# Moving eight modulation blocks from the norm stops into the FFN loops of a two-model program

## The reference, cut to what matters

```python
m_lat = jnp.split((silu_c @ w_mod[i] + b_mod[i])[:, None, :], N_MOD, axis=-1)      # N_MOD = 9
m_ctx = jnp.split((silu_cc @ w_mod[i] + b_mod[i])[None, None, :], N_MOD, axis=-1)

def swiglu(u, w_in, w_out):
    a, v = jnp.split(u @ w_in, 2, axis=-1)
    return (jax.nn.silu(a) * v) @ w_out

def ffn_sublayer(h, shift, scale, gate, w_in, w_out, g, b):
    y = swiglu(modulate(h, shift, scale), w_in, w_out)
    return layer_norm(ALPHA * h + FFN_RES * gate * y, g, b)

def ada_modulation(cond, w_ada, b_ada):                                            # the second model
    m = (jax.nn.silu(cond) @ w_ada + b_ada)[:, None, :]
    return jnp.split(m, 6, axis=-1)
```

## Time and profile before

| | before |
|---|---|
| median of 3 runs | 2881.59 us (2879.3 to 2887.91) |
| profiled execution, its own time | 2883.8 us |
| its span in the trace | 2882.1 us |
| granted TensorE clock, mean | 0.954 of full |
| PE busy | 2612.0 us, 91% |
| weight loads (beside PE) busy | 1885.5 us, 65% |
| DVE busy | 1523.2 us, 53% |
| ACT busy | 894.8 us, 31% |
| POOL busy | 221.8 us, 8% |
| L1974 splits on DVE | 392, 477.6 us |
| L2013 multiply-adds on DVE | 210, 259.8 us |

### The profile page before, as it was taken

How to read it: one execution, slowest core, us unless ns; L and a number is a source line. 1 busy time by engine, 2 the same in 40 slices (tenths; PEclk the granted TensorE clock), 3 DMA queues, 4 the chain that set the end, 5 groups by cost and what they waited for, 6 DMA issues and landing times. The chain is left out here.

```text
span 2882.1 us, 39680 instructions
## 1 busy us (share of the span) xinstructions
PE 2612.0 (91%) x14422; PEld 1885.5 (65%) x14422; DVE 1523.2 (53%) x2305; ACT 894.8 (31%) x1421; POOL 221.8 (8%) x372
## 2 busy tenths in 40 slices
PE   5999997998999999999999878997988998798987
PEld 3878874665687887687876647996666433466322
DVE  3855754444576576675676556566543232563101
ACT  2222224443322222422224444445333100443100
POOL 0000103231010000100010001000001000000000
PEclk9999998998999999999999989998998999899999
DMA  7655545232475454654555206664104699515998
GB/s 265 195 163 148 171 141 139 73 74 72 148 211 172 137 172 150 210 183 144 162 186 171 66 27 208 187 180 122 56 15 194 285 426 428 177 47 241 405 428 348
DMA packets 428844, 527.78 MB, mean 183 GB/s; under 512 B 29766, under 2 KB 382532, under 8 KB 416292
## 3 DMA queue, kind: packets, MB, share of 16 engines
q1 hardware_dynamic: 393188, 399.71, 40.4%
q0 software_dynamic: 35520, 126.24, 13.8%
HBM read 524.85 MB, written 1.05 MB: 182 GB/s over the span
## 5 line engine op out<-in xcount | busy, mean ns | idle before, releaser
L1974 DVE TENSOR_TENSOR wlo<-raw,whi 128x1024 fp32r<-128x1024 f32 x392 | 477.6, 1222 | 298.0 <-ACT whi L1492 277.2
L1492 ACT ACTIVATE whi<-raw 128x1024 fp32r<-128x1024 f32 x392 | 413.9, 1057 | 588.0 <-PE bank L714 527.2
L712 PE MATMUL bank<-xhi,whi 128*128 128x512 f32 (+1 forms) x1568 | 575.0, 367 | 3.0 <-DVE xlo L2539 3.0
L713 PE MATMUL bank<-xlo,whi 128*128 128x512 f32 (+1 forms) x1568 | 565.8, 361 | 0.0
L714 PE MATMUL bank<-xhi,wlo 128*128 128x512 f32 (+1 forms) x1568 | 565.2, 360 | 0.0
L712 PEld LDWEIGHTS bank<-xhi,whi 128*128 128x128 f32 x1568 | 298.3, 190 | 65.5 <-issue 22.4
L714 PEld LDWEIGHTS bank<-xhi,wlo 128*128 128x128 f32 x1568 | 298.1, 190 | 45.1
L713 PEld LDWEIGHTS bank<-xlo,whi 128*128 128x128 f32 x1568 | 298.7, 191 | 43.5 <-issue 0.7
L2013 DVE SCALAR_TENSOR_TENSOR acc<-mod_ring,conds,acc 128x1024 f32<-128x1024 f32 x210 | 259.8, 1279 | 7.7 <-DMA mod_ring<-in_w_ada 3.4
L1368 PE MATMUL bank<-experts,gathered 128*64 128x512 f32 (+1 forms) x1024 | 236.6, 617 | 28.9 <-DMA experts<-in_w_up 25.9
L712 PE MATMUL bank<-hhi,whi 128*128 128x512 f32 (+1 forms) x704 | 256.4, 364 | 0.2 <-DVE hlo L2121 0.2
(11 more groups left out here) (323 smaller groups left out, 3363.0 us busy)
## 6 DMA issues: line engine op xcount, KB each, us to landing
raw<-in_ffn_w_in SPq DMA_DIRECT2D x176, 512.0 KB, 4.0
mod_ring<-in_w_mod POOLq DMA_DIRECT2D x128, 512.0 KB, 4.8
experts<-in_w_gate SPq DMA_DIRECT2D x32, 2048.0 KB, 20.7
experts<-in_w_up SPq DMA_DIRECT2D x32, 2048.0 KB, 20.2
experts<-in_w_down SPq DMA_DIRECT2D x32, 2048.0 KB, 21.0
mod_ring<-in_w_ada POOLq DMA_DIRECT2D x96, 512.0 KB, 5.0
raw<-in_ffn_w_out SPq DMA_DIRECT2D x64, 384.0 KB, 3.3
raw<-in_ffn_w_out SPq DMA_DIRECT2D x64, 320.0 KB, 3.2
```

Of the source, the lines that this page charges most:

```text
L712: pe.matmul(o, wh, hi[:, k0 + k, cols], start=(first and k == 0), stop=False)
L713: pe.matmul(o, wh, lo[:, k0 + k, cols], start=False, stop=False)
L1492: act.activation(whi[:, slot, :], raw[:, slot, :], ACT.Copy).then_inc(*n.mark("hi_ready"))
L1974: dve.tensor_tensor(wlo[:, slot, :], raw[:, slot, :], whi[:, slot, :].bitcast(F32), ALU.subtract)\
```

## The change

The fillers are taken out of all engines. Their eight blocks (six of two conditions, two of one) become riders on DVE, most of them in the down loops, which carried none. `RIDERS` now has four lists for each FFN: up and down of half 0, up and down of half 1. A down loop that carries a block is written out as one piece of two or four iterations instead of a hardware loop of four. `SLICES` gets an entry for four repetitions, and blocks of one repetition put their eight slices after the first two splits, four and four. On POOL, the attention bias no longer stands behind 16 filler transfers.

```diff
-RIDERS = (((("w_mod", 0, 2, 2, 2, 2), ("w_ada_2", 1, 3, 1, 1, 1)), (("w_mod", 0, 4, 2, 2, 2), ("w_ada_2", 1, 4, 1, 1, 1))),
-          ((("w_mod", 1, 1, 2, 2, 2), ("w_mod", 1, 7, 1, 1, 1)), (("w_ada_2", 1, 0, 2, 2, 2), ("w_ada_2", 1, 2, 1, 1, 1))),
-          ((("w_ada_2", 0, 0, 2, 2, 2), ("w_mod", 1, 8, 1, 1, 1)), (("w_ada_2", 0, 3, 2, 2, 2), ("w_ada_2", 1, 5, 1, 1, 1))),
-          ((("w_ada_2", 0, 2, 1, 0, 1), ("w_ada_2", 0, 5, 1, 0, 1)), ()))
-SLICES = {1: (3, 3, 2, 0), 2: (1, 2, 1, 2, 1, 1, 0, 0)}
+RIDERS = (
+    ((("w_mod", 0, 2, 2, 2, 2), ("w_ada_2", 1, 3, 1, 1, 1)), (("w_mod", 0, 6, 1, 2, 4),),
+     (("w_mod", 0, 4, 2, 2, 2), ("w_ada_2", 1, 4, 1, 1, 1)), (("w_mod", 0, 7, 1, 2, 4),)),
+    ((("w_mod", 0, 8, 1, 2, 2), ("w_mod", 1, 0, 1, 2, 2), ("w_mod", 1, 7, 1, 1, 1)), (("w_mod", 1, 3, 1, 2, 2), ("w_mod", 1, 5, 1, 1, 2)),
+     (("w_mod", 1, 1, 2, 2, 2), ("w_ada_2", 1, 2, 1, 1, 1)), (("w_mod", 1, 4, 1, 2, 4),)),
+    ((("w_ada_2", 1, 0, 2, 2, 2), ("w_mod", 1, 8, 1, 1, 1)), (("w_ada_2", 0, 3, 1, 2, 2), ("w_mod", 1, 6, 1, 1, 2)),
+     (("w_ada_2", 0, 0, 2, 2, 2), ("w_ada_2", 1, 5, 1, 1, 1)), (("w_ada_2", 0, 4, 1, 2, 4),)),
+    ((("w_ada_2", 0, 2, 1, 0, 1), ("w_ada_2", 0, 5, 1, 0, 1)), (), (), ()))
+SLICES = {1: (4, 4, 0, 0), 2: (1, 2, 1, 2, 1, 1, 0, 0), 4: (1, 0, 1, 0, 1, 1, 0, 1, 0, 1, 1, 0, 1, 0, 0, 0)}
 MACS_AHEAD = 8
-FILLERS = ((("w_mod", 0, 6), ("w_mod", 0, 7)), (("w_mod", 0, 8), ("w_mod", 1, 0)), (("w_mod", 1, 3), ("w_mod", 1, 4)), (("w_mod", 1, 5), ("w_mod", 1, 6)))
...
     yield "up", 0, 0, 1, 1, None
     for half, (_, nf) in enumerate(HALVES):
-        first, last = 1 - half, nf // 2
-        for name, l, block, times, conds, reps in riders[half]:
-            yield "up", half, first, times, reps, (name, l, block, conds)
-            first += times * reps
-        assert first <= last
-        if first < last:
-            yield "up", half, first, last - first, 1, None
-        yield "down", half, 0, KD // 2, 1, None
+        for kind, first, last, ridden in (("up", 1 - half, nf // 2, riders[2 * half]), ("down", 0, KD // 2, riders[2 * half + 1])):
+            for name, l, block, times, conds, reps in ridden:
+                yield kind, half, first, times, reps, (name, l, block, conds)
+                first += times * reps
+            assert first <= last
+            if first < last:
+                yield kind, half, first, last - first, 1, None
...
-            fillers, fill_no = [], [0]
-
-            def fill(steps=2 * KD):
-
-                for _ in range(steps):
-                    if not fillers:
-                        return
-                    name, j, k = fillers.pop(0)
-                    if k == 0:
-                        acquire(6 + j)
-                    pe.wait_ge(*n.next(f"mod_full{k % MOD_RING}", 16))
-                    mod_step(6 + j, k, mod_ring[:, k % MOD_RING, :], name)
-
-            def turn_fillers(rows):
-
-                for b, row in zip((6, 7), rows):
-                    evacuated(b)
-                    pe.sem_inc(s[f"bank_ready{b}"], 1)
-                    acquire(b)
-                    passed()
-                    turn_row(b, row)
...
-            def layer_norm(cols, steps):
-
-                if fill_no[0] < len(FILLERS):
-                    fillers.extend((name, j, k) for j, (name, _, _) in enumerate(FILLERS[fill_no[0]]) for k in range(KD))
-                    fill_no[0] += 1
-                fill(steps[0])
+            def layer_norm(cols):
+
                 pe.wait_ge(*n.next("h_ready"))
                 acquire(4)
                 pe.matmul(bank[4][:, cols], tab("mean_d"), hsum[:, cols], start=True, stop=True).then_inc(s["bank_ready4"], 1)
-                fill(steps[1])
-                inverse_root(cols, steps[2])
-                fill(steps[3])
+                inverse_root(cols)
 
...
-                    own_steps = 2 * reps if kind == "up" else 2 * more + 2 * adding
+                    own_steps = 2 * reps if kind == "up" else (2 * more + 2 * adding) * reps
...
-                                residual(f, m, gate, i * 2 + (2 * start + f), cols)
+                                k = i * (2 * reps) + (2 * (start + rep) + f)
+                                residual(f, m, gate, k, cols)
                                 if adding:
-                                    add_tile(i * 2 + (2 * start + f), cols)
+                                    add_tile(k, cols)
                                 continue
...
             pool.memset(vrow[:, :, :], 0.0).then_inc(s["zeroed"], 1)
             ride(RIDERS[0])
-            ride_fillers(0)
             ring_read()
 
             pool.wait_ge(*n.next("inputs_loaded", N_LOADS * 16))
             pool.wait_ge(*n.next("x_ready", 2 * KD))
-            n.next("bank_read7", sum(times for half in RIDERS[0] for _, _, _, times, _, _ in half) + 2)
+            n.next("bank_read7", sum(times for half in RIDERS[0] for _, _, _, times, _, _ in half))
 
             rpb = a["rpb"]
...
             pool.wait_ge(*n.peek("bank_read7"))
-            ride_fillers(1)
             ride(RIDERS[1])
-            ride_fillers(2)
             ride(RIDERS[2])
-            ride_fillers(3)
             pool.wait_ge(*n.next("h_ready", 5))
             rows = a["ctx_2"][0].rearrange("(t p) (q c) -> t p q c", p=P, c=S)
```

More of the change, by code:

```diff
@@ L295, in build @@
     hm = at("hm", [P, KD, T], F32, big + 48 * KB)
-    product_rows = [hm[:, j, 0:MOD_COLS // 4] for j in range(2)]
-    fill_rows = [tmp[:, 2, j * MOD_COLS // 4:(j + 1) * MOD_COLS // 4] for j in range(2)]
     mrow = at("mrow", [P, MOD_COLS // 4], F32, big + 48 * KB)
@@ L519, in up_down @@
                                 k0 = f0 + part * (nf // 2)
-                                unit(wo[:, k0:k0 + nf // 2, ds(i * 256 + (2 * start + d) * P, P)], nf // 2 * P)
+                                unit(wo[:, k0:k0 + nf // 2, ds(i * (256 * reps) + (2 * (start + rep) + d) * P, P)], nf // 2 * P)
             def columns(w, tiles):
@@ L840, in up_down, with inverse_root @@
                             mod_turn()
-            def inverse_root(cols, between=0):
+            def inverse_root(cols):
                 tiles = range(cols.stop // P)
@@ L852, in inverse_root @@
                             mm.then_inc(s[f"square_sum{c}"], 1)
-                fill(between)
                 pe.wait_ge(*n.next("root_ready"))
@@ L1551, in modulated, with up_down @@
                 input_of(h, lambda k, g: mcol(m, scale, k, g), lambda k, g: mb[:, k, g:g + 1], cols)
-            def filler_rows(rows):
-                for b, row in zip((6, 7), rows):
-                    for q in range(4):
-                        act.wait_ge(*n.next(f"mod_used{q}", KD))
-                    act.activation(row, bank[b][:, 0:MOD_COLS // 4], ACT.Copy).then_inc(*n.mark(f"bank_read{b}"))
-                    n.next(f"bank_read{b}")
-            def up_down(cols, riders, next_loads=(), after_norm=True):
+            def up_down(cols, riders, next_loads=()):
                 for kind, half, start, times, reps, rider in ffn_loops(riders):
@@ L1566, in up_down @@
                     last = next_loads and (kind, half) == ("down", 1)
-                    for runs in (times - 1, 1) if last else (times,):
-                        if last and runs == 1:
-                            loads.extend(next_loads)
+                    assert not last or times == 1
+                    for runs in (times,):
                         with n.loop(act, runs, strides(reps, **{f"bank_read{b}": reps for b in used}, **{f"bank_read{b}": 1 for b in [6, 7] * m},
@@ L1573, in up_down @@
                                 f = step_no % 2
+                                if last and step_no == 2 * reps - 2:
+                                    loads.extend(next_loads)
                                 units(1)
@@ L1576, in up_down @@
                                     mod_row(on_dve)
-                                if f and after_norm and (kind, half, start) == ("up", 0, 0):
-                                    filler_rows(product_rows)
                                 units(1)
@@ L1626, in neighbourhood @@
                     move(0, b)
-                filler_rows(fill_rows)
                 exp(0)
@@ L2015, in row_slices @@
                         n.next("row_summed", 4)
-            def fillers(i):
-                for b, filler in zip((6, 7), FILLERS[i]):
-                    n.next(f"bank_read{b}")
-                    mod_columns(b, *filler)
-                    ring_passed()
             def first_mods(i):
@@ L2076, in residual, with up_down @@
                         .then_inc(*n.mark(f"bank_read{b}" if last else "dve"))
-            def up_down(cols, m, gate, riders, norm, gate_rides=False, new_context=False, filler=None):
+            def up_down(cols, m, gate, riders, norm, gate_rides=False, new_context=False):
                 scale_residual(cols, *norm)
@@ L2125, in up_down @@
                             mod_columns(7, *rider[0:2], i + rider[2])
```

(15 more changed lines are left out.)

26 lines of the change are left out of this document (9 added, 17 removed).

## The result

| | before | after |
|---|---|---|
| median | 2884.75 us (4 runs, 2879.3 to 2888.76) | 2853.77 us (4 runs, 2847.28 to 2863.23) |
| profiled execution | 2883.8 us, span 2882.1 | 2847.28 us, span 2845.6 |
| ratio of the times | | 0.9896, 95% interval 0.9862 to 0.9931 |

The change makes the kernel 31 us, 1.1%, faster. The forecast was 2859.5 (2847 to 2874), 25 us under the new median of before. In a later run beside other kernels the ratio was 0.9865 (0.9847 to 0.9884).

What follows compares the result with a forecast made beforehand. TensorE (PE) was taken as the bound inside the FFN loops, with waits for DVE and the bias elsewhere. Terms -22.0 + 11.4 + 4.8 - 11.5 - 4.8 = -22.1 gave 2861.7 profiled, 2859.5 us median, range 2847 to 2874.

Steps and rivals of the forecast that it cites:

- D: Stop 0: the attention bias no longer waits behind filler transfers on POOL, -11.5 us (-9 to -12).
- A: Six one-repetition blocks: most of PE's row-sum wait for DVE goes, with slow products after it; -22.0 us (-10 to -24).
- B: FFN loops: small matmuls and turns of eight more blocks on PE, without cover, +11.4 us.
- C: Two half-0 down loops: PE waits 1.7 us for DVE and loses 0.7 by the clock; +4.8 us (0 to +9).
- E: Four stops: earlier first products and no filler work, against a slower clock (2.2 us in stop 1); -4.8 (-10 to +4).
- rival 5: Better case: no stall in the half-0 down loops and the whole gain of the one-repetition blocks; 2852 us, chance 0.10.
- rival 1: One-repetition blocks: ring slots land too late for the eighth multiply-add, gain only -10, total 2871.5 us; chance 0.13.
- rival 2: Clock falls in all stops without fillers, stops gain near 0.9, total -18 us, 2863.5 us; chance 0.12.
- The slower rival: DVE becomes the bound of the down loops; with 1.2 us lost a tile +41, total 2900 us; chance 0.07.

Runs made afterwards that it cites:

- e1: Changed kernel with the one-repetition blocks back at the old order 3, 3, 2, 0; 2870.69 us, ratio to before 0.9955.
- e2: Kernel before with only the order 4, 4, 0, 0 in one-repetition blocks, fillers kept; 2868.16 us, ratio to before 0.9946.
- e4: Changed kernel with the one-condition block first in the half-0 down loops of the second and third FFN; 2850.35 us.
- e3: Changed kernel with ten more memsets on POOL, each waiting for the one before, ahead of the attention bias; 2859.70 us.
- e7: Kernel before with order 4, 4, 0, 0 and only stop 0's two blocks made riders, the other six staying fillers; 2860.46 us, ratio to before 0.9892.
- e5: Changed kernel with unread matmuls, seven in each norm stop of the first model, three at each of the second model's two; 2839.61 us.
- e6: Changed kernel with the eight pairs of four-repetition blocks one behind each of the first eight splits instead of spread over sixteen; 2861.27 us.
- e8: Changed kernel with three unread matmuls inside a stop and seven before the first product, these seven also at the second model's two stops; 2840.59 us.
- e9: Changed kernel with three unread matmuls inside a stop and seven before the first product, these seven not at the second model's stops; 2840.97 us.

## Why the prediction was right, term by term

Differences between the traces of before and after, the first two and the second two. The loops are measured from the hidden tile ahead of them to the next hidden tile or the mean matmul of the norm, D from stop 0's mean matmul to PE's first matmul behind the softmax:

| term | forecast | measured | second pair |
|---|---|---|---|
| A, six one-repetition blocks | -22.0 | -22.6 | -20.5 |
| B, eight blocks more on PE in the loops | +11.4 | +10.8 | +10.8 |
| C, DVE short in two half-0 down loops | +4.8 | +3.0 | +3.0 |
| D with stop 0 of E | -10.7 | -11.0 | -11.9 |
| E, stops 1 to 3 with the attentions | -5.7 | -10.8 | -14.3 |
| places without an edit in the first model | 0 | -2.0 | -0.5 |
| the rest | 0 | -4.0 | -2.8 |
| sum | -22.2 | -36.6 | -36.2 |

The range held and terms A to D came out within 2 us each. The sum was short by 14 us: 5 in E, 6 in places that no edit touches, which the forecast put at nothing, and the others in C, A, B and D. Against the 22 us forecast stand 36 by the traces and 31 by the medians, and that the median came within 6 us of 2859.5 is in part luck: before itself was 3 us slower here than in the three runs that the forecast started from. The median also lies near rival 5's 2852, but not for its reason, since the wait of C was there.

**A** is the block by block difference from the tile before the sum to the tile behind: 3.7, 4.6, 4.3, 3.3, 4.2 and 2.5. The order did it, as e1 and e2 show from both sides. The end of the last multiply-add was forecast for 182.1 and came at 182.56, by the ring that rival 1 named: its slot took 6.1 us, not 5.5. The waits that stayed are 0.5 us a block at most, in the second trace once 0.83, so rival 1's mechanism exists at a tenth of its price. What the forecast had from one trace and took for fixed is the part of the clock: 7.0 us in before, 3.2 in e1.

**B and C**: a half-0 down loop with one block grew by 0.8, its turn fell into the next up loop, 1.0, together 1.8 against 1.71. A half-1 down loop grew by 0.9 to 1.0 instead of 1.2. The wait of C was forecast at 1.7 and is 1.52 in both loops; the 0.7 for a slower clock behind it didn't come. Its cause was wrong, as e4 shows: not the late start but DVE's work behind the second split.

**D** came out where it was put, and e3 prices it separately. Inside it the chain on POOL took 13.6 us from the memset to the last addition (453.44 to 467.06), not 11.4 and up to 1.5 more, and it still ended 0.16 us ahead of the scores; a slower chain would have shown in the time.

**E was mis-sized.** Of the 5.1 us between forecast and the first pair, 3.0 lie in layer 0's attention and 2.2 in stops 1 to 3. The first is chance. The output projection of that attention began with products of 0.79 and 0.63 us in before and of 0.49 and 0.39 in after, behind the same wait, and in the second traces it was the other way round (before and its second trace, then after and its second trace):

```profile
712.99 0.79 PE L712 MATMUL bank<-aohi,whi 128*128 128x512 f32 x1 [1.84 <-DVE aolo L2245]
712.39 0.49 PE L712 MATMUL bank<-aohi,whi 128*128 128x512 f32 x1 [1.85 <-DVE aolo L2245]
695.31 0.49 PE L712 MATMUL bank<-aohi,whi 128*128 128x512 f32 x1 [1.85 <-DVE aolo L2189]
696.54 0.79 PE L712 MATMUL bank<-aohi,whi 128*128 128x512 f32 x1 [1.84 <-DVE aolo L2189]
```

Stops 1 to 3, with layer 1's attention, gained 7.8 us in the first pair and 15.3 in the second, and the e7 kernel, which keeps the fillers there, needed 10.3 to 13.7 us more than the changed one. So fillers cost PE's path about twice the 5.7 us that I had added up from tails and late starts. Part of what I left out is the ring: in stop 1 of before PE stood six times for a slice between its filler steps, 5.9 us in all, with the norm's own matmuls behind them in the queue. The first two:

```profile
764.29 0.64 PE L677 MATMUL bank<-mod_ring,conds 128*32 128x256 f32 x8 [1.73 <-DMA mod_ring<-in_w_mod]
765.57 1.08 PE L677 MATMUL bank<-mod_ring,conds 128*32 128x256 f32 x8 [0.65 <-DMA mod_ring<-in_w_mod]
```

How much of those waits the norm would have waited anyway was not measured.

**The clock in the stops.** The 2.2 us charged in stop 1, and rival 2, rest on fillers that keep the clock up. The traces of before show this in one stop only: its stop 1 began at 0.50 us a product, but stops 0, 2 and 3, and all four in its second trace, began at 0.80 and 0.63 right behind the filler matmuls, and the second trace's stop 1 was 2.9 us longer. In the changed kernel all four begin at 0.76 or 0.77. So there was little clock to lose. By the section What's actually happening of "TensorE: Matmul & The Clock Gate" in the Trainium skill the clock follows PE's recent work. e5, which adds work that nobody reads and is 11 us faster, agrees. It doesn't decide between fillers and no fillers here: e7 keeps them and is slower.

**The slower rival** didn't happen: in the spread half-1 loops DVE is at 91% and PE waits for nothing. e6 shows how near it was, with the same work and another table. Its price in the prediction doesn't add up: 34 is the number of tiles with two conditions, 40 carry multiply-adds, and at 3.4 us for each 0.1 us the gain of 22 would be gone with 0.65 us over PE's tile, not 0.9, and lost twice with 1.3, not 1.9.

## What to carry to other kernels

When a slower engine's result gates PE, look at the order on that engine before its load: six blocks gained 20.5 to 22.6 us against before (14.0 against e1) by two instructions moved ahead, with no work less, and the same work bunched in another place cost 11 us in three loops. Follow each queue past the operation that is removed: a third of this gain was a bias on POOL that stood behind transfers for another engine. And time in which PE must wait before a run of products can be filled with matmuls that nobody reads: seven in a stop gained 11 us here, and ten no more than seven. Before a gain is put down to a place, compare two traces of the same kernel there: layer 0's attention moved by 3 us between traces with no edit.

## What the runs showed of the hardware that was not expected

The rest of the program, the same instructions in every kernel but e5, e8 and e9, took 900.5 to 913.3 us, and the three kernels that were traced twice kept their value within 2.2 us. Granted clock in the 30 us that begin 135 us behind the last norm (span, PE busy, clock), for after, before and e7:

```profile
2080.06:2110.06 30.00, 21.18 (x107) 0.94 0.00 1
```

```profile
2112.56:2142.56 30.00, 21.19 (x107) 0.97 0.00 1
```

```profile
2082.84:2112.84 30.00, 22.45 (x100) 0.89 0.00 1
```

In e7 PE was busy longer over fewer matmuls, 100 against 107, at a lower granted clock, and in its second trace too (23.49 us, 0.89). The order of before and after is not as firm: second traces had 22.35 us at 0.94 and 21.19 at 0.97. The lag of e7 behind the changed kernel stood at 0.9 us before this place, 4.2 behind it, and grew again to 11 some 610 to 660 us behind the last norm. What sets it, in a part of the program away from any edit, was not found; the kernels with fillers had 904.5 to 913.3 and the eight without 900.5 to 905.8, which is no proof. Nor is it known how much of the 31 us it holds: 2.8 to 4.0 us in the two pairs of traces. For a change of a few us it means that the trace up to a common point says more than the total.
